# Splitting a top-16 routing look-up into a part for ranks 1 to 8 and a part for ranks 9 to 16

## What is computed

```
v1, i1 = top_k(s1, 16); v2, i2 = top_k(s2, 16)          # s1, s2: (T, 8, 128) scores
cand = (v1[..., :, None] + v2[..., None, :]).reshape(T, 8, 256)
sc, ci = top_k(cand, 16)
e = take_along_axis(i1, ci // 16) * 128 + take_along_axis(i2, ci % 16)
g = softmax(sc)
act = einsum('td,tkd->tk', x, u_tab[e]);  out = einsum('tk,tkd->td', gelu(act) * g, v_tab[e])
```

## Time and profile before

| | |
|---|---|
| median of 3 runs | 1817.09 us (1816.93 to 1817.82) |
| the profiled execution | 1817.6 us, of which its span is 1815.6 us |
| busy, of the span | TensorE 93%, VectorE 87%, ScalarE 42%, GpSimd 38% |
| routing stage, first to last `place` | 397 to 575 us |
| tail of the routing | 575 to 586 us |
| one-hot stage | 586 to 716 us |
| expert stage | from 730 us to the end |

### The profile page before, as it was taken

One profiled execution on the slowest core, in us unless ns is written; L12 is line 12 of the kernel. 1 busy time (PEld: TensorE's weight loads), 2 busy tenths in 40 slices (PEclk: granted clock), 3 DMA queues, 4 the chain that ended last, 5 costly groups with the idle time before them and its releaser, 6 DMA issues.

```text
span 1815.6 us, 28944 instructions
## 1 busy us (share of the span) xinstructions
PE 1692.0 (93%) x9360; PEld 1420.6 (78%) x9360; DVE 1577.9 (87%) x3181; ACT 767.1 (42%) x1653; POOL 686.8 (38%) x611
## 2 busy tenths in 40 slices
PE   6999988999963887799999999999999999999997
PEld 4566766955542787699989999998999999999986
DVE  2687852488889997799999999999999999999998
ACT  3122563330002888344444444444444444444443
POOL 0000000035565887344344444434343444444441
PEclk9999999999885999899999999999999999999999
DMA  8443102211112478999999999999999999999996
GB/s 318 140 142 137 47 1 73 70 59 58 35 35 93 140 228 256 367 398 388 392 405 400 400 401 398 414 390 394 408 406 395 409 393 404 404 410 399 394 392 211
DMA packets 128781, 508.71 MB, mean 280 GB/s; under 512 B 8528, under 2 KB 63568, under 8 KB 79312
## 3 DMA queue, kind: packets, MB, share of 16 engines
q0 software_dynamic: 36864, 268.45, 36.8%
q1 hardware_dynamic: 91568, 239.34, 35.2%
q10 hardware_dynamic: 288, 0.13, 0.0%
HBM read 479.97 MB, written 27.92 MB: 280 GB/s over the span
## 4 chain that ended last, share of the span: by engine, by line
DVE 35%; DMA 23%; PE 21%; issue 18%; POOL 1%; ACT 1%; DVEq 1%; POOLq 0%; SPq 0%; ACTq 0%
DMA slab<-table,ixr 21%; DVE slab L1452 8%; PE psum L413 7%; DVE ulo L1368 4%; PE psum L619 3%; DVE slab L1406 3%; DVE slab L1444 3%; PE psum L706 2%; DVE vlo L1431 2%; PE psum L414 2%; DVE slab L1439 2%; DVE wlo L1427 1%; POOL slab L1534 1%; PE psum L550 1%; DVE slab L1410 1%
## 5 line engine op out<-in xcount | busy, mean ns | idle before, releaser
L1534 POOL DMA_INDIRECT slab<-table,ixr x256 | 426.0, 1664 | 604.0 <-DVE slab L1452 554.3
L727 PE MATMUL psum<-hhi,uhi 128*128 128x384 f32 x1008 | 340.1, 337 | 7.4 <-issue 7.1
L1452 DVE SCALAR_TENSOR_TENSOR slab<-slab,cf 128x1024 f32<-128x1024 f32 x256 | 328.5, 1283 | 15.1 <-DVE slab L1452 0.5
L1444 DVE SCALAR_TENSOR_TENSOR slab<-slab,h2tok 128x1024 f32<-128x1024 f32 x256 | 312.3, 1220 | 33.5 <-DMA slab<-table,ixr 33.3
L727 PE MATMUL psum<-hhi,ulo 128*128 128x384 f32 x1008 | 339.0, 336 | 0.0
L727 PE MATMUL psum<-hlo,uhi 128*128 128x384 f32 x1008 | 338.5, 336 | 0.0
L741 PE MATMUL psum<-vhi,whi 128*128 128x512 f32 x768 | 299.6, 390 | 14.2 <-DVE wlo L1427 13.9
L741 PE MATMUL psum<-vhi,wlo 128*128 128x512 f32 x768 | 301.8, 393 | 0.0
L741 PE MATMUL psum<-vlo,whi 128*128 128x512 f32 x768 | 301.5, 393 | 0.0
L413 PE MATMUL psum<-slab 128*128 128x512 f32 x464 | 246.6, 614 | 7.9 <-ACT slab L862 5.2
L727 PEld LDWEIGHTS psum<-hhi,uhi 128*128 128x128 f32 x1008 | 190.0, 188 | 17.3 <-issue 12.8
(11 more groups left out here) (207 smaller groups left out, 2696.3 us busy)
## 6 DMA issues: line engine op xcount, KB each, us to landing
slab<-ublk SPq DMA_DIRECT2D x64, 1024.0 KB, 8.6
slab<-vtab SPq DMA_DIRECT2D x64, 1024.0 KB, 8.5
slab<-wblk SPq DMA_DIRECT2D x90, 512.0 KB, 4.1
slab<-g_dram SPq DMA_DIRECT2D x32, 768.0 KB
g_dram<-slab SPq DMA_DIRECT2D x11, 2048.0 KB, 7.5
slab<-table,ixr POOLq DMA_INDIRECT x256, 9.6
x<-x_in SPq DMA_DIRECT2D x1, 2560.0 KB, 9.4
y_out<-x SPq DMA_DIRECT2D x5, 512.0 KB, 3.5
```

Of the source, the lines that this page charges most:

```text
L727: last = pe.matmul(psum[:, b, 0:ND], w[:, c, :], m[:, c, :], start=(m_ == 0), stop=(m_ == 3 * DC - 1))
L1444: v.scalar_tensor_tensor(out=rows[:, sl % GR, 0:D], in0=rows[:, sl % GR, 0:D], scalar=1.0, in1=h2tok[:, k, :], op0=ALU.mult, op1=ALU.mult, ...
L1452: v.scalar_tensor_tensor(out=accs[k][:, e, :], in0=rows[:, sl % GR, D:2 * D], scalar=cf[:, sl:sl + 1], in1=accs[k][:, e, :], op0=ALU.mult, ...
L1534: pool.indirect_dma_start(out=rows[:, sl % GR, :], out_offset=None, in_=table, in_offset=bass.IndirectOffsetOnAxis(ap=ixr[:, half, sl % 8: ...
```

## The change

`RUNS` still names the 50 candidates for the sums. Two new lists, `EARLY_RUNS` (20 candidates that can hold ranks 1 to 8) and `LATE_RUNS` (the other 30), set the order of `eid` and of `count`. `place`, `hit` and `half` are split in two: an early part of 20 candidates by picks 0 to 7, and a late part of all 50 candidates by picks 8 to 15. The constants get 50 more columns, which hold the place of each candidate in the order of `RUNS` (`rank_ranges`). The early part is multiplied and folded for all tiles in one instruction each, the late part tile by tile as before. The long line that declares semaphores gains `valued_early` and `folded_early` and is left out.

```diff
@@ -57,6 +57,22 @@
 RUNS = [(0, 1, 16), (1, 1, 8), (2, 1, 5), (3, 1, 4), (4, 1, 3), (5, 3, 2), (8, 8, 1)]
 CAND = sum(n * w for _, n, w in RUNS)
+EARLY = TOP // 2
+EARLY_RUNS = [(0, 1, 0, 8), (1, 1, 0, 4), (2, 2, 0, 2), (4, 4, 0, 1)]
+LATE_RUNS = [(0, 1, 8, 16), (1, 1, 4, 8), (2, 1, 2, 5), (3, 1, 2, 4), (4, 1, 1, 3), (5, 3, 1, 2), (8, 8, 0, 1)]
+ID_RUNS = EARLY_RUNS + LATE_RUNS
+N_EARLY = sum(n * (w1 - w0) for _, n, w0, w1 in EARLY_RUNS)
+def rank_ranges():
+    starts = {i: sum(TOP // (r + 1) for r in range(i)) for i in range(TOP)}
+    at = [starts[i] + j for i0, n, w0, w1 in ID_RUNS for i in range(i0, i0 + n) for j in range(w0, w1)]
+    rank = [(i + 1) * (j + 1) for i0, n, w0, w1 in ID_RUNS for i in range(i0, i0 + n) for j in range(w0, w1)]
+    assert sorted(at) == list(range(CAND)) and all((r <= EARLY) == (k < N_EARLY) for k, r in enumerate(rank))
+    return at
 RING = 4
 N_ADA1, N_IN, N_ADA2, N_PW, N_OUT, N_WQ, N_ADA3 = 16, 14, 24, 4, 8, 16, 8
@@ -87,13 +103,14 @@
 V_NORM1, V_NORM2, V_BADA, V_COND, V_QG, V_KG, V_CW, V_CB, V_LG, V_LB, V_SINK = 0, 8, 16, 64, 80, 81, 82, 206, 210, 214, 218
 V_END = V_SINK + HEADS
-C_ID, C_SEL, C_ROT, C_MASK, C_IOTA, C_SUM, C_COS, C_SIN, C_END = 0, 128, 130, 258, 898, 1026, 1028, 1540, 2052
+C_ID, C_SEL, C_ROT, C_MASK, C_IOTA, C_SUM, C_COS, C_SIN, C_AT = 0, 128, 130, 258, 898, 1026, 1028, 1540, 2052
+C_END = C_AT + CAND
...
 GSTEPS = SLOTS // 16
-NUMBER_STEPS = 2 + len(RUNS)
+NUMBER_STEPS = 2 + len(ID_RUNS)
 HEAD_STEPS = 2 * 5 * TILES + len(RUNS) + 5 * TILES + 2
...
@@ -205,14 +222,16 @@
         best, besti = view(21504, TILES, 2, TOP), view(21664, TILES, 2, TOP).bitcast(U32)
         scr = view(25344, 2, TILES, P)
-        hit = view(13824, TILES, CAND, TOP)
-        place = view(22784, TILES * TOP * CAND // 2).bitcast(BF16).rearrange("p (t n k) -> p t n k", t=TILES, n=CAND)
+        hit_early, hit_late = view(13824, TILES, N_EARLY, EARLY), view(14624, TILES, CAND, EARLY)
+        place_early, place_late = (view(c0, TILES * EARLY * n // 2).bitcast(BF16).rearrange("p (t n k) -> p t n k", t=TILES, n=n)
+                                   for c0, n in ((22784, N_EARLY), (23184, CAND)))
+        half_early, half_late = view(22784, TILES, EARLY, N_EARLY // 2), view(23184, TILES, EARLY, CAND // 2)
         cand, cand2, eid = view(17824, TILES, CAND), view(18080, TILES, CAND), view(35456, TILES, CAND)
-        hit_last = view(35712, N_GATHER, CAND, TOP)
-        half, half_last = view(22784, TILES, TOP, CAND // 2), view(37312, N_GATHER, TOP, CAND // 2)
+        last_early, last_late = view(35712, N_GATHER, N_EARLY, EARLY), view(36032, N_GATHER, CAND, EARLY)
+        half_last_early, half_last_late = view(37312, N_GATHER, EARLY, N_EARLY // 2), view(37472, N_GATHER, EARLY, CAND // 2)
         ex = view(18608, TILES, PH, TOP)
-        count = view(19248, CAND * TOP // 2).bitcast(BF16).rearrange("p (n k) -> p n k", n=CAND)
+        count = view(19248, CAND * EARLY // 2).bitcast(BF16).rearrange("p (n k) -> p n k", n=CAND)
         accs = (view(9216, 2, D), view(23552, 2, D))
         e1u, e2u = (view(33792 + n, ND).bitcast(U32) for n in (0, ND))
...
@@ -690,7 +709,7 @@
             pe.wait_ge(h2_tok, 2 * N_GATHER)
             for k in range(N_DENSE):
                 pe.wait_ge(picked, 1)
-                pe.wait_ge(dense_looked, k + 1)
+                pe.wait_ge(dense_looked, 2 * (k + 1))
                 pe.transpose(psum[:, k, 0:P], ef[:, N_GATHER + k, :], ident)
                 pe.transpose(psum[:, k, P:2 * P], gw[:, N_GATHER + k, :], ident).then_inc(by_slot, 1)
@@ -1270,8 +1289,10 @@
             def numbers(i):
+                v.wait_ge(folded_early, i)
+                v.tensor_reduce(ef[:, :, bass.ds((i - 1) * TOP, EARLY)], half_early, AX_X, ALU.add).then_inc(looked, 1)
                 v.wait_ge(folded, i * TILES)
-                v.tensor_reduce(ef[:, :, bass.ds((i - 1) * TOP, TOP)], half, AX_X, ALU.add).then_inc(looked, 1)
+                v.tensor_reduce(ef[:, :, bass.ds((i - 1) * TOP + EARLY, EARLY)], half_late, AX_X, ALU.add).then_inc(looked, 1)
             def search(i, first):
@@ -1337,15 +1358,17 @@
                 if not first:
                     numbers(i)
                     v.wait_ge(valued, i * TILES)
-                    v.wait_ge(looked, i)
+                    v.wait_ge(looked, i * 2)
                 tk(v.tensor_copy(topf[:], topi[:]))
                 own()
-                each = [P, TILES, CAND, TOP]
-                v.tensor_tensor(place, count.unsqueeze(1).broadcast_to(each), topf[:].unsqueeze(2).broadcast_to(each), ALU.is_equal).then_inc(found, 1)
+                for place, n, k0 in ((place_early, N_EARLY, 0), (place_late, CAND, EARLY)):
+                    each = [P, TILES, n, EARLY]
+                    v.tensor_tensor(place, count[:, 0:n].unsqueeze(1).broadcast_to(each), topf[:, :, k0:k0 + EARLY].unsqueeze(2).broadcast_to(each),
+                                    ALU.is_equal).then_inc(found, 1)
...
-            v.tensor_copy(count, con[:, C_IOTA:C_IOTA + CAND].unsqueeze(2).broadcast_to([P, CAND, TOP])).then_inc(topk_step, 1)
+            v.tensor_copy(count, con[:, C_AT:C_AT + CAND].unsqueeze(2).broadcast_to([P, CAND, EARLY])).then_inc(topk_step, 1)
             search(0, True)
             with v.Fori(1, PH) as i:
                 search(i, False)
@@ -1355,22 +1378,25 @@
             def tried_numbers(k):
                 t = N_GATHER + k
-                v.tensor_tensor(hit[:, t], place[:, t], eid[:, t, :].unsqueeze(2).broadcast_to([P, CAND, TOP]), ALU.mult).then_inc(tried, 1)
+                for hit, place, n in ((hit_early, place_early, N_EARLY), (hit_late, place_late, CAND)):
+                    v.tensor_tensor(hit[:, t], place[:, t], eid[:, t, 0:n].unsqueeze(2).broadcast_to([P, n, EARLY]), ALU.mult).then_inc(tried, 1)
             def dense_numbers(k):
                 t = N_GATHER + k
-                v.wait_ge(tried, k + 1)
-                v.tensor_reduce(ef[:, t, (PH - 1) * TOP:PH * TOP], hit[:, t].rearrange("p n k -> p k n"), AX_X, ALU.add).then_inc(dense_looked, 1)
+                for part, hit in enumerate((hit_early, hit_late)):
+                    at = (PH - 1) * TOP + EARLY * part
+                    v.wait_ge(tried, 2 * k + part + 1)
+                    v.tensor_reduce(ef[:, t, at:at + EARLY], hit[:, t].rearrange("p n k -> p k n"), AX_X, ALU.add).then_inc(dense_looked, 1)
             def u_rest(n, jj):
                 v.wait_ge(uhi_set, n + 1)
                 v.tensor_tensor(ulo[:, jj % 4], uraw[:, jj // 2 % 2, jj % 2], uhi[:, jj % 2].bitcast(F32), ALU.subtract).then_inc(ulo_set, 1)
             exh = ex.rearrange("p t h k -> p (t h) k")
-            v.wait_ge(found, PH)
+            v.wait_ge(found, 2 * PH)
             v.wait_ge(number_step, PH * NUMBER_STEPS)
-            v.wait_ge(looked, PH - 1)
+            v.wait_ge(looked, 2 * (PH - 1))
             tried_numbers(0)
             v.wait_ge(exped, 1)
             step(v.tensor_reduce(den[:], exh, AX_X, ALU.add))
@@ -1410,10 +1436,12 @@
                     v.tensor_tensor(hot_a[:, b % 4, m0:4, :], con[:, C_IOTA:C_IOTA + KEYS].unsqueeze(1).broadcast_to(wide),
                                     e1T[:, col:col + 4 - m0].unsqueeze(2).broadcast_to(wide), ALU.is_equal).then_inc(hot_b_set, 1)
                 if k == 0:
+                    v.wait_ge(folded_early, PH)
                     v.wait_ge(folded, TILES * (PH - 1) + N_GATHER)
-                    v.tensor_reduce(ef[:, 0:N_GATHER, (PH - 1) * TOP:PH * TOP], half_last, AX_X, ALU.add)\
-                        .then_inc(looked, 1)
-                    v.wait_ge(looked, PH)
+                    for part, half in enumerate((half_last_early, half_last_late)):
+                        at = (PH - 1) * TOP + EARLY * part
+                        v.tensor_reduce(ef[:, 0:N_GATHER, at:at + EARLY], half, AX_X, ALU.add).then_inc(looked, 1)
+                    v.wait_ge(looked, 2 * PH)
                     step(v.tensor_copy(idxu[:, 0:N_GATHER], ef[:, 0:N_GATHER]))
                     settle()
                     for n in range(2):
@@ -1491,7 +1519,7 @@
             pool.memset(scond[:], 0.0).then_inc(cond_zero, 1)
             pool.memset(ones[:], 1.0).then_inc(ones_set, 1)
-            def look_up(i, tiles, hit, half):
+            def look_up(i, tiles, hit_early, hit_late, half_early, half_late):
                 pool.wait_ge(ranked, i + 1)
                 pool.sem_inc(paced_pool, 1)
                 pool.tensor_copy(bestf[:], besti).then_inc(number_step, 1)
@@ -1500,23 +1528,30 @@
                 pool.tensor_scalar(bestf[:, :, 0, :], bestf[:, :, 0, :], float(KEYS), None, ALU.mult).then_inc(number_step, 1)
                 pool.wait_ge(number_step, i * NUMBER_STEPS + 2)
                 at = 0
-                for i0, rows_, w in RUNS:
+                for i0, rows_, w0, w1 in ID_RUNS:
+                    w = w1 - w0
                     shape = [P, TILES, rows_, w]
```

(21 more changed lines are left out.)

## The result

The changed kernel takes 1804.36 us (median of 6, 1801.92 to 1808.74) against 1817.45 us before (median of 6, 1815.74 to 1820.86): a ratio of 0.9933, 95% interval 0.9922 to 0.9945, or 12.2 us less, with 10.0 to 14.2 us inside the interval.

A forecast was written before the change was run, and what follows sets the result against it. VectorE alone was taken to set the routing stage's pace, 25.07 us a head. Gains of 9.35 us less a 1.07 us wait for the Exp made 8.3 us: 1808.8 us from the median 1817.1, range 1806.0 to 1812.0.

The forecast's parts named there:

- the 0.17 of the one-hot stage: Gathered tiles' last sum (line 1414): 560 elements in two instructions instead of 800, gain 0.17 us.
- one spot: Loop gap on VectorE from the candidate sums to the next max, 1.27 us before; the forecast left it unchanged.
- the wait for the Exp: Tail: VectorE's sum of the exponentials would newly wait 1.07 us for ScalarE's Exp, cutting 9.35 to 8.3 us.
- `numbers`: Candidate sums in the loop on VectorE, 400 + 1000 elements instead of 2000: gain 0.544 us, seven times, 3.81 us.
- a dense pair of sums: Tail, line 1364, three sums: 560 elements instead of 800 at 1.67 ns each, gain 3 x 0.32 = 0.97 us.
- The register operations: Loop: one more wait, `folded_early`, per `numbers`, its register operation charged in full: 7 x 0.07 = 0.49 us.
- The dense products: Tail, line 1358, three products: 160 + 400 elements, 0.74 us for 0.91, gain 0.51 us.
- costed at nothing: GpSimd's look-ups would not delay VectorE in the loop; possible 1.6 us lateness in the tail kept only for the range.
- The packed rate: Rival: `place` with rows of 8 falls to one element a step, net +2.3 us, 1819.4 us; chance 0.05.
- rival 3: Expert stage: the earlier start leaves one more single gather open, 10.2 us, eating the gain, 1819.0 us; chance 0.05.
- Rival 4: Tail: no wait for the Exp, so the gain is 9.35 us, 1807.7 us; chance 0.15, inside the range.
- The rule set against the sum: Trainium skill: next instruction starts only when the pipe is empty; each added one costs 0.157 us, gain near 6.8 us.

The follow-up runs named there:

- the repeat: The changed kernel run again unchanged: ratio 0.9936, 11.6 us less; the kernel before was also run again unchanged: ratio 1.0001.
- four_parts: Changed kernel with the look-up in four parts of four picks, against 8, 20, 36 and 50 candidates: ratio 0.9917 to the kernel before, median 1802.02 us.
- four_one_wait: The four-part look-up with only the last fold raising VectorE's semaphore, so one register operation ahead of the sums goes: ratio 0.9929, median 1804.4 us.
- pad_before: The kernel before with one idle semaphore increment on VectorE's queue at the start of each pass over heads: 1815.25 us, run once.
- quiet_tail: The changed kernel with GpSimd's last look-up held back until VectorE has finished the three dense tiles: 1809.35 us, one execution.
- split_all: The kernel before with its look-up in two parts but nothing left out, both comparing with all 50 candidates: ratio 1.0012.

## Why the prediction was wrong, point by point

The traced gain of routing and tail is 11.3 us where 8.1 were foretold (8.3 without the 0.17 of the one-hot stage). Of the 3.2 us between them the loop has 2.4 and the tail 0.9. The step that failed is therefore first what stands between the instructions of the loop, which the sum charged with 0.49 us and which gave 1.7 (0.56 from a register operation and 1.1 from one spot), and second the wait for the Exp. The Exp alone would not have done it: without it the sum was 1807.7 us, inside the range. From the median before, 11.3 us less would be 1805.8 to 1806.2 us, at the range's lower end. So the traced gain alone brings the time to the edge of the range; the remaining 0.9 of the 12.2 us is less than the interval is wide (the repeat had 11.6), and no run shows where it lies.

- **What bounds the kernel, and that the gain passes to the end: right.** TensorE and GpSimd never hold VectorE in the loop, and neither the one-hot nor the expert stage is longer or shorter beyond its scatter.
- **The elements: right.** `place` gained 0.55 us (0.547 foretold), `numbers` 0.57 (0.544), a dense pair of sums 0.29 (0.32), the last sum of the gathered tiles 1.01 - 0.83 = 0.18 (0.17). An added instruction costs 0.07 us (0.077).
- **The register operations: the largest miss beside the spot. 0.49 us charged, 0.56 gained.** No operation was added. In the kernel before one stands ahead of the sum (line 1273 in the order rows, at 470.02 in the trace); its heir, line 1294, runs at 467.61 under the first sum, because `folded_early` is awaited at the counter itself. The second sum starts 0.49 us after the first, which leaves 0.07 beyond its 400 elements. So the operation costs nothing there, and its 0.08 us ahead of the first sum are saved in each head. The order rows in front of the prediction show this, but the charge counts line 1294 as an addition. four_parts and four_one_wait test it.
- **The spot in the loop: taken as fixed**, 7 x 0.12 + 0.24 = 1.1 us. The row left out of the earlier trace rows showed it. The loop's gain is thus 7.15 + 0.49 + 0.56 + 1.1 + 0.2 (the 0.03 us a head by which `numbers` beat its price) = 9.5 us, as measured.
- **The wait for the Exp, 1.07 us foretold, none measured: the second step that failed.** I shifted ScalarE's chain by 6.67 us as if its length were fixed. It holds four loads of weights, and its length wanders: from the start of TensorE's line 401 to the start of the Exp there were 14.21 us in the profile I read, 13.47 in its repeat and 12.73 in pad_before, all with the old look-up, and 12.81 and 12.63 in the changed kernel. TensorE stood still for the loads for 4.15 us of the longest and 2.88 of the changed kernel's. My 0.2 us of cover came from the longest of all eleven; in the repeat it was 0.97. After the change:

```profile
564.98 1.28 ACT L955 ACT_TABLE_LOAD   x1
566.27 0.74 ACT L955 ACTIVATE slab<-slab 128x640 f32<-128x640 f32 x1
```

  The Exp ended at 567.01 and the sum started at 567.69, as soon as the slow products ahead were done. With a chain of 14.21 us the Exp would have ended at 568.4, 0.7 us after that (an estimate); that no wait came was luck. Where the products are not slow, the cover is gone: 566.37 and 566.40 in quiet_tail (from its ScalarE row at 565.63), and 0.3 us of waiting in four_one_wait. So the mechanism is there, and what it cost at most was 0.3 us.
- **The dense products: 0.51 us foretold, a loss of 0.95 measured, and a gain of 1.35 beside it that nobody foretold.** In the kernel before GpSimd's last look-up met another instruction with two inputs, the scaling of the weights:

```profile
578.94 2.30 POOL L1512 TENSOR_TENSOR slab<-slab 128x800 f32<-128x800 bf16 x1
```
```profile
578.82 1.01 DVE L1358 TENSOR_TENSOR slab<-slab 128x800 f32<-128x800 bf16 x1
579.75 2.17 DVE L1382 TENSOR_TENSOR gw<-slab,den 128x640 f32<-128x640 f32 x1
581.84 1.51 DVE L1364 TENSOR_REDUCE ef<-slab 128x16 f32<-128x800 f32 x1
```

  The scaling takes 2.09 us from start to start; it is 0.74 now (571.55 to 572.29), because GpSimd's last fold ends at 571.2 and only clears a buffer after it. The old products were not slowed, since they started first (578.82, GpSimd's 578.94) and GpSimd's had to wait. I read these collisions only from GpSimd's side. That 1.46 us too much and 1.35 too little nearly cancel is luck. Tail, with the last `place` and the three dense sums: 0.55 - 0.95 + 1.35 + 0.87 = 1.8 us, against 0.96 foretold.
- **GpSimd: costed at nothing, rightly in the loop** and wrongly in the tail, as above. In the loop the cover I named was too large. Not `numbers` at 494 us but the candidate additions at 488.9 come first, and meeting them costs 0.41 us a head.
- **The rivals.** The packed rate held with rows of 8 and of 4. No stage behind the routing grew beyond its scatter, as rival 3 would have had it. Rival 4 was the right one for the Exp.
- **The rule set against the sum.** The section "The DRAIN you can't avoid" of the Trainium skill's page "VectorE: DVE Perf Modes" goes on to say that a next instruction that is not held starts earlier. The prediction left that out. The traces agree: 0.07 us for an added instruction in split_all, not 0.157.
- **A small slip**: the signs put the first line 1406 row near 578.4; the prediction's own terms ahead of that row give 578.55. It came at 576.36.
- **The range** allowed for a mistake on the low side in the Exp and the dense sums alone. And I had taken the scatter from three executions that lay within 0.9 us; ten of the same kernel later went from 1813.3 to 1822.4 us, and the medians of its later groups of runs from 1816.3 to 1817.5.

Open is what the spot in the loop is. VectorE was idle there for 0.50 us in the first pass and 0.27 in the others, and no run here looks at why.

## What to carry to other kernels

Count elements and instructions by steps from start to start: in the loop that part of the sum was right to 0.03 us a head. Then compare the register operations ahead of each wait, before and after. A cover read from one execution is worth nothing if the chain behind it holds DMA loads; take its length from two profiles before charging a wait. And when VectorE's instructions with two inputs can meet GpSimd's work, ask which pair meets before and which after, and which of the two starts first.

## What the runs showed of the hardware that I had not expected

- An idle semaphore increment at the top of a loop body made seven passes 1.1 us shorter in one kernel (175.73 to 174.64) and 0.1 longer in another (166.13 to 166.24).
- A GpSimd instruction stretches VectorE's two-input instructions and not its one-input ones: 560 elements in two products took 0.66 to 0.76 us alone and 1.27 to 1.70 in company, and 640 elements of line 1382 before took 2.09 us against 0.74 for the same line after (1408). Beside GpSimd's clearing of a buffer (571.14 to 572.95) the 0.74 us stayed 0.74.
- In the other direction too: GpSimd's product of 800 elements took 1.55 us alone and 2.28 beside VectorE's, and VectorE's own product, which had started 0.12 us earlier, took 0.99 us (0.97 in the third, which met no such work).
